# A two-block transformer kernel: the end and the start of the experts' weight stream reordered, and its last slabs cut into several transfers

## The reference

```python
def _moe(h, router_w, router_b, w_gate, b_gate, w_up, b_up, w_down, b_down):
    logits = (h @ router_w + router_b)                 # 256 x 32 experts
    top_logit, top_e = lax.top_k(logits, TOP_K)        # 4 experts for a token
    top_w = jax.nn.softmax(top_logit, axis=-1)
    ...
    def expert_block(args):
        xe, e = args
        gate = jnp.minimum(xe @ w_gate[e] + b_gate[e], 7.0)
        up = jnp.clip(xe @ w_up[e] + b_up[e], -7.0, 7.0)
        act = (up + 1) * (gate * jax.nn.sigmoid(1.702 * gate))
        return act @ w_down[e] + b_down[e]
    ...
    y = yb[dest] * sorted_w[:, None]
    return jax.ops.segment_sum(y, sorted_tok, num_segments=t)
```

## Time and profile before

| what | value |
|---|---|
| median of 3 runs | 1879.58 us (1879.22 to 1886.42) |
| the profiled execution, first to last instruction | 1879.4 us |
| TensorE busy | 1788.0 us, 95% |
| VectorE busy | 669.4 us, 36% |
| ScalarE busy | 575.4 us, 31% |
| transfers | 563.18 MB, 300 GB/s over the span |
| chain that ended last | PE 76%, DMA 18%, DVE 3%, ACT 2% |

### The profile page before, as it was taken

One profiled execution on the slowest core, in us unless ns is written; L12 is line 12 of the kernel. 1 busy time (PEld: TensorE's weight loads), 2 busy tenths in 40 slices (PEclk: granted clock), 3 DMA queues, 4 the chain that ended last, 5 costly groups with the idle time before them and its releaser, 6 DMA issues.

```text
span 1879.4 us, 24354 instructions
## 1 busy us (share of the span) xinstructions
PE 1788.0 (95%) x10246; PEld 1086.8 (58%) x10246; DVE 669.4 (36%) x1211; ACT 575.4 (31%) x1042; POOL 20.1 (1%) x59
## 2 busy tenths in 40 slices
PE   5999999999999999999999999989999999989999
PEld 4987787333333333333323233268799997779998
DVE  2654664111111111111111111154655455655454
ACT  4445573101101100110101011045554445555443
POOL 0010010000000000000000000000000000000000
PEclk9999999999999999999999999999999999999999
DMA  8664547999999999999999999974455464325450
GB/s 308 242 218 174 192 180 319 407 427 426 427 428 427 427 428 426 426 427 428 428 427 427 427 426 428 427 284 157 135 173 186 159 220 143 128 90 189 170 202 23
DMA packets 122048, 563.18 MB, mean 300 GB/s; under 512 B 7216, under 2 KB 53424, under 8 KB 97360
## 3 DMA queue, kind: packets, MB, share of 16 engines
q1 hardware_dynamic: 121104, 558.70, 74.4%
q10 hardware_dynamic: 832, 2.89, 0.4%
HBM read 560.52 MB, written 1.05 MB: 299 GB/s over the span
## 4 chain that ended last, share of the span: by engine, by line
PE 76%; DMA 18%; DVE 3%; ACT 2%; issue 1%; SPq 0%; ACTq 0%; DVEq 0%
PE ps L1093 15%; PE ps L660 12%; PE ps L661 12%; PE ps L662 12%; PE ps L1116 10%; DMA arena<-in_w_up 9%; DMA ring<-in_w_up 7%; PE ps L1051 2%; PE ps L1031 2%; DMA ring<-in_w_ada 1%; PE ps L672 1%; PE ps L979 1%; DMA ring<-in_w_in 1%; PE ps L765 1%; PE ps L1012 1%
## 5 line engine op out<-in xcount | busy, mean ns | idle before, releaser
L660 PE MATMUL ps<-part,part 128*128 128x256 f32 (+2 forms) x1592 | 512.0, 322 | 7.9 <-DVE part L1998 5.0
L661 PE MATMUL ps<-part,part 128*128 128x256 f32 (+2 forms) x1592 | 502.0, 315 | 0.0
L662 PE MATMUL ps<-part,part 128*128 128x256 f32 (+2 forms) x1592 | 501.7, 315 | 0.0
L1998 DVE TENSOR_TENSOR part<-ring,part 128x1024 fp32r<-128x1024 f32 (+2 forms) x299 | 313.2, 1089 | 122.4 <-ACT part L1455 121.8
L660 PEld LDWEIGHTS ps<-part,part 128*128 128x128 f32 (+1 forms) x1592 | 304.3, 191 | 42.0 <-issue 13.6
L662 PEld LDWEIGHTS ps<-part,part 128*128 128x128 f32 (+1 forms) x1592 | 304.0, 191 | 19.3
L661 PEld LDWEIGHTS ps<-part,part 128*128 128x128 f32 (+1 forms) x1592 | 304.4, 191 | 17.1
L1455 ACT ACTIVATE part<-ring 128x1024 fp32r<-128x1024 f32 (+2 forms) x299 | 271.9, 948 | 34.6 <-PE ps L662 18.9
L1093 PE MATMUL ps<-ring,arena 128*64 128x512 f32 x1216 | 269.9, 595 | 10.9 <-DMA ring<-in_w_up 9.4
L1995 DVE TENSOR_SCALAR arena<-ps 128x512 f32<-128x512 f32 x64 | 44.2, 691 | 428.1 <-PE ps L1093 428.1
L1093 PEld LDWEIGHTS ps<-ring,arena 128*64 128x64 f32 x1216 | 84.2, 137 | 193.7 <-issue 169.1
(11 more groups left out here) (254 smaller groups left out, 1218.0 us busy)
## 6 DMA issues: line engine op xcount, KB each, us to landing
ring<-in_w_down SPq DMA_DIRECT2D x39, 2048.0 KB, 35.6
ring<-in_w_up SPq DMA_DIRECT2D x38, 2048.0 KB, 36.0
ring<-in_w_gate SPq DMA_DIRECT2D x38, 2048.0 KB, 35.0
arena<-in_w_up SPq DMA_DIRECT2D x26, 2048.0 KB, 36.9
ring<-in_ffn_w_in SPq DMA_DIRECT2D x44, 1024.0 KB, 7.8
arena<-in_w_down SPq DMA_DIRECT2D x18, 2048.0 KB, 37.0
spare<-in_w_gate SPq DMA_DIRECT2D x13, 2048.0 KB, 35.4
arena<-in_w_gate SPq DMA_DIRECT2D x13, 2048.0 KB, 34.7
```

Of the source, the lines that this page charges most:

```text
L660: e.matmul(out, x[0], y[0], start=first, stop=False, skip_group_check=True)
L661: e.matmul(out, x[0], y[1], start=False, stop=False, skip_group_check=True)
L662: return e.matmul(out, x[1], y[0], start=False, stop=last, skip_group_check=True)
L1998: return e.tensor_tensor(out, x, y, op)
```

## The change

- **First slab.** 0.g0 raises `s_used` four times, once for each of its four rows of weights (k = 0 to 3), and the load that takes its slot, 1.d0, is four transfers of one row each (128 partitions of 4 KB, 512 KB), each waiting for its row.
- **Order.** Expert 31's g0, u0, g4, u4 are loaded before expert 30's d0 and d4, and PE runs them in that order: for expert 30, `turn_act` is followed by `turn_gathered(31)` and all of `gate_up(31)`, then by d0 and d4. DVE evicts expert 30's down result after expert 31's activation. Expert 31's gate and up slabs count on a signal of their own.
- **Last slabs.** 31.g4, 31.u4 and 31.d0 are each loaded as five transfers: one of 96 partitions and four of 8 partitions. 31.d4 is four transfers of one row each, with a signal for each, and PE waits for each row by itself.
- **`begin_sum`** moves from expert 0 to expert 27, behind `put_back(26)`; the first `put_back` starts the sums in its place.

```diff
@@ plan_rows
             src = w[128 * k0:128 * k0 + 512, :].rearrange("(p k) n -> p k n", k=4)
-            plan(key, 4, D, lambda ap: [(ap, src)], slot)
+            n = 1 if user[slot] == first_used or key == last_used else 4
+            if key in (("moe_g", NE - 1, 4), ("moe_u", NE - 1, 4), ("moe_d", NE - 1, 0)):
+                cuts = (0, 96, 104, 112, 120, 128)
+                plan(key, 4, D, lambda ap: [(ap[x:y], src[x:y]) for x, y in zip(cuts, cuts[1:])], slot)
+                return
+            plan(key, 4, D, lambda ap: [(ap[:, k:k + n, :], src[:, k:k + n, :]) for k in range(0, 4, n)], slot)
@@ order of the loads
         for ex in range(NE):
+            if ex < NE - 1:
+                plan_gate_up(ex)
+            if ex == NE - 2:
+                plan_gate_up(NE - 1)
             for k0 in (0, 4):
                 plan_rows(("moe_d", ex, k0), A["w_down"][0][ex], k0, next(order))
@@ sync_program
-                for to, src in pairs:
-                    e.dma_start(to, src).then_inc(s_slot[slot].sem, 16)
+                for n, (to, src) in enumerate(pairs):
+                    if before == first_used:
+                        e.wait_ge(*s_used.of("gate", 0, n))
+                    e.dma_start(to, src).then_inc(s_last_row[n].sem if key == last_used else s_slot[slot].sem, 16)
@@ tensor_program
+                    if ex < NE - 1:
+                        gate_up(ex)
                     if ex:
                         put_back(ex - 1)
                     else:
-                        begin_sum()
+                        e.wait_ge(*s_pickTe.of())
+                    if ex == 27:
+                        begin_sum(False)
                     if ex + 1 < NE:
                         gather(ex + 1)
                     turn_act(ex)
+                    if ex == NE - 2:
+                        turn_gathered(NE - 1)
+                        gate_up(NE - 1)
                     for k0 in (0, 4):
                         w = ("moe_d", ex, k0)
-                        if k0 and ex + 1 < NE:
+                        if k0 and ex + 1 < NE - 1:
                             turn_gathered(ex + 1)
                         e.wait_ge(*s_ate.of(ex, k0 // 4))
-                        e.wait_ge(*loaded(w))
+                        if w != last_used:
+                            e.wait_ge(*loaded(w))
                         for k in range(4):
+                            if w == last_used:
+                                e.wait_ge(s_last_row[k].sem, 16)
@@ vector_program
+                    if ex == NE - 1:
+                        e.wait_ge(*s_put.of(ex - 2))
+                        e.wait_ge(*s_used.of("down", ex - 1, 4))
+                        evict_down(ex - 1)
```

More of the change, by code:

```diff
@@ L223, in plan @@
             pairs = pairs_of(ap)
-            in_slot[slot] += 16 * len(pairs)
+            if key != last_used:
+                in_slot[slot] += 16 * len(pairs)
             loads.append((key, pairs, slot, user[slot]))
@@ L258, in build, with used, using @@
         s_slot = [signal(f"slot{i}_loaded", 16) for i in range(NSLOT + 4)]
-        s_used = signal("weights_used")
+        s_last_row = [signal(f"last_row{k}_loaded", 16) for k in range(4)]
+        s_used, s_used_end = signal("weights_used"), signal("last_gate_up_used")
+        def used(kind, ex, k0):
+            return (s_used_end if ex == NE - 1 and kind != "down" else s_used).of(kind, ex, k0)
+        def using(kind, ex, k0):
+            return (s_used_end if ex == NE - 1 and kind != "down" else s_used).up(kind, ex, k0)
         def W(key):
@@ L426, in build, with plan_gate_up @@
         user[7], user[8], user[9] = ("tiles", 7), ("tiles", 8), ("tiles", 9)
-        for ex in range(NE):
+        def plan_gate_up(ex):
             for k0 in (0, 4):
@@ L431, in build @@
                     plan_rows(("moe_u", ex, k0), A["w_up"][0][ex], k0, next(order))
+        for ex in range(NE):
+            if ex < NE - 1:
+                plan_gate_up(ex)
+            if ex == NE - 2:
+                plan_gate_up(NE - 1)
             for k0 in (0, 4):
@@ L621, in rel @@
                 return [s_wlo.of("a", max(t for t, x in enumerate(a_pieces) if x[0] == key))]
-            if kind in ("moe_g", "moe_u"):
-                return [s_used.of("gate" if kind == "moe_g" else "up", key[1], key[2])]
-            if kind == "moe_d":
-                return [s_used.of("down", key[1], key[2])]
+            if key == first_used:
+                return []
+            if kind in ("moe_g", "moe_u", "moe_d"):
+                return [used({"g": "gate", "u": "up", "d": "down"}[kind[-1]], key[1], key[2])]
             return [s_wlo.of(last_of[key])]
@@ L991, in turn_weights, with begin_sum @@
                 i.then_inc(*s_pickT.up())
-            def begin_sum():
+            def begin_sum(first):
                 e.wait_ge(*s_pickTe.of())
@@ L998, in begin_sum @@
                     for h in range(2):
-                        e.matmul(b.Y[q][h], b.wT[:, 128 * q:128 * q + 128], bdn[:, 512 * h:512 * h + 512], start=True, stop=False,
+                        e.matmul(b.Y[q][h], b.wT[:, 128 * q:128 * q + 128], bdn[:, 512 * h:512 * h + 512], start=first, stop=False,
                                      skip_group_check=True)
@@ L1082, in tensor_program, with project @@
                     xg, aT = b.xg, b.aT
[L1083 to L1089 removed]
+                    def project(n, r, k0):
+                        w, bank = ("moe_" + "gu"[r], n, k0), (6 if n % 2 == 0 else 4) + r
                         e.wait_ge(*loaded(w))
@@ L1092, in project, with gate_up @@
                             for h in range(2):
-                                i = e.matmul(PS[p + r][CAP * h:CAP * h + CAP, :], xg[:, k0 + k, :],
+                                i = e.matmul(PS[bank][CAP * h:CAP * h + CAP, :], xg[:, k0 + k, :],
                                              W(w)[:, k, 512 * h:512 * h + 512], start=False,
                                              stop=k0 == 4 and k == 3, skip_group_check=True)
-                        i.then_inc(*s_used.up(("gate", "up")[r], ex, k0))
-                    for k0 in (0, 4):
-                        for r in range(2):
-                            project(r, k0)
+                            if w == first_used:
+                                i.then_inc(*s_used.up("gate", 0, k))
+                        if w != first_used:
+                            i.then_inc(*using(("gate", "up")[r], n, k0))
+                    def gate_up(n):
+                        e.wait_ge(*s_xge.of(n))
+                        if n:
+                            e.wait_ge(*s_pwe.of(n))
+                            biases(n)
+                        for k0 in (0, 4):
+                            for r in range(2):
+                                project(n, r, k0)
+                    if ex < NE - 1:
+                        gate_up(ex)
                     if ex:
@@ L1124, in tensor_program @@
                 turn_weights()
-                begin_sum()
+                begin_sum(True)
                 for h in range(2):
@@ L2390, in vector_program @@
                         w = ("moe_d", ex, k0)
-                        e.wait_ge(*loaded(w))
+                        if w != last_used:
+                            e.wait_ge(*loaded(w))
+                        else:
+                            for k in range(4):
+                                e.wait_ge(s_last_row[k].sem, 16)
                         tt(W(w), W(w), b.gm.unsqueeze(1).to_broadcast([128, 4, D]), ALU.mult).then_inc(*s_dclip.up("down", ex, k0))
```

31 lines of the change are left out of this document (14 added, 17 removed).

## The result

The changed kernel takes **1916.2 us** (1911.76 to 1919.72, 4 runs) for 1881.0 of the kernel before in the same comparison (1879.22 to 1886.42): ratio **1.0173**, interval 1.0151 to 1.0194. It is 1.7% slower. Forecast were 1875.3, with 1879.7 as the upper end.

What follows compares the result with a forecast made beforehand. Slab transfers were taken to set the time from mid-stream to its end. 4.3 us from the stream plus 0.7 from the order minus 0.7 lost behind gave 1879.6 - 4.3 = 1875.3 us, range 1871.0 to 1879.7.

Steps and rivals of the forecast that it cites:

- The cuts of 96 and 8: Last slabs 31.g4, 31.u4, 31.d0: small pieces shift packets between engines, landings up to 3.7 us sooner or later; PE gains nothing.
- The small pieces cost, slower: Rival, last stretch: twelve small transfers each hold the queue 2.8 us, 31.d0 lands 33.6 later; 1907 us, chance 0.05.
- What would show it: List of signs in the trace; a rate well under 427 GB/s from 1190 to 1225 would mean pieces that cost.
- begin_sum: Moved from expert 0 to 27: later slots come free 3.3 us sooner at the front; cost 0 at expert 27.
- the stream's 4.3: Experts' weight stream: with both early gaps in the landings closed, it is 4.3 us sooner; bounds 2.8 to 5.6.
- First slab by rows: Start of the stream: 1.d0 issued row by row, 2.75 us sooner; landings of 1.d4, 2.g0, 2.u0 move by 1.4 us.
- The last slabs' order: End of the MoE: PE's idle time falls from 2.86 to 2.2 us, gain 0.7; the end then bound by PE.

Runs made afterwards that it cites:

- first ladder: Changed kernel with whole last slabs and one up slab cut at each of eight experts, a different shape each; one execution took 1963.6 us.
- experiment 10: Three kernels; the one for `begin_sum` is the kernel before with only that sum moved from expert 0 to expert 27: 1878.4 us, ratio 0.9987.
- experiment 1: Changed kernel with 31.g4, 31.u4 and 31.d0 loaded whole again, all else of the change kept: 1881.52 us, ratio 0.9996.
- experiment 7: Changed kernel with whole last slabs and six up slabs cut: every fourth, eighth, sixteenth partition, a middle piece, 112 + 16, halves; 1961.74 us.
- experiment 8: Changed kernel with whole last slabs and up slab 0 of six experts each cut into two halves of 64 partitions: 1936.45 us.
- the ladders: Two runs of the changed kernel with whole last slabs and single up slabs cut in eight, then six, shapes: 1963.6 and 1961.74 us.

## Why the prediction was wrong

- **"The cuts of 96 and 8"** is the step that failed. It counted packets, two more or two less for an engine and slab, and put 0 us into the forecast. It took for granted that a packet takes the same 0.61 us in whatever pieces the slab is cut. In the trace the engines stayed busy and moved half, at 1.27 us a packet. Measured: 34.7 us (1916.2 - 1881.5, from two comparisons whose kernels before are 1.8 apart), the whole loss.
- **The rival "The small pieces cost, slower"** had the side and, by chance, the size (1907, 32 us), from a wrong mechanism: a fixed time for each piece. Halves without a small piece cost 25.9 us, sixteen small pieces in the first ladder no more than two large ones. It got 0.05, because landings 4.9 us apart "for whole transfers" were held against it. That row says nothing of transfers that aren't whole, and there was none in the trace: a missing row was read as a price of 0. The bound from above had to come from this rival, and the range should have reached to it.
- **What would show it** named the sign rightly: "a rate well under 427 from 1190 to 1225".
- ***begin_sum*** moved the later issues nearly as foretold (2.g4 is issued 21.4 us behind g0, foretold 21.1, before 24.4), and at expert 27 cost nothing visible. What came of it at the end of the MoE is less than the stream's 4.3: 2.5 us in its own kernel (experiment 10).
- ***First slab by rows***: foretold 1.4 us, measured 0 to 0.1. In experiment 1 the four rows are issued from 324.15 to 326.72, 4.2 to 7.8 us ahead of their landings, and the last is in at 326.72 + 7.8 = 334.5, where the whole slab landed at 334.6. 1.d4 then lands 9.4 us after its issue at 330.15, at 339.6 for 339.5. The forecast had it land after 7.7. Without these 1.4 the forecast's front is 4.3 - 1.4 = 2.9 us; from g0 to the landing of 30.u4 the stream gained 2.8 (see the result).
- ***The last slabs' order***: foretold 0.7, measured 0.2 with the rows of 31.d4. PE's wait for ACT came as foretold (0.96 for 0.95). But the end isn't "bound by PE then": in experiment 1 PE still waits 1.24 us for 30.d4, as it did for 31.u4 before. The forecast's sum had no landing in it there (30.d4 was to be in at 1220.4 "at the worst", for a PE that would come later). The wait moved to another slab.
- **The whole without the cuts** gains 912.4 - 910.0 = 2.4 us in experiment 1's profile, for 4.3 in the forecast; its median is 1.2 under its comparison's, which can't be told from 0.

What stays open: whether the packets slow at the writing side, as the ports have it, or at the reading side (experiment 7), and why a cut into halves costs more than its own slab at half rate (4.9 us; measured 6.6 to 18.9). Transfers beside it that are whole slow down too (31.u0 and 30.d4 in the result), and the price rises from cut to cut (experiment 8). Engines that stand at different places of the queue, so that each slows another's whole transfer, would do both; that 31.u0 is late, though it stands ahead of every cut slab, fits it. The records don't name a packet's engine or partition, so this is argued, not shown.

## What to carry to other kernels

If a transfer into SBUF (the core's memory of 128 partitions) has to be cut, cut it along its free axis, within the partitions, or take every second or fourth partition; a cut into runs of partitions cost 7 to 19 us a slab of 2 MB here, in a queue that was the bound. When a rate halves while the engines' share stays at 1, the packets have become slower: look at what they hold, and not for gaps or fixed costs. And where a shape of transfer has no row in the trace, its price is unknown and not 0: the range has to reach to the worst rival, however small its chance.

## What the runs showed of the hardware

- A transfer of every fourth partition costs nothing extra, every eighth 6.5 us a slab of 2 MB, every sixteenth 17.0, at an engine share of 1.0 in each.
- Pieces of one row (128 partitions x 4 KB) are free in the middle of the stream (425 GB/s), and gain nothing at its dry start.
- The price of a cut depends on the cuts before it: 6.6 to 11.0 us over six alike, and 11.9 and 18.9 in the ladders.
- Whole slabs beside cut ones are late too: 31.u0, ahead of the first cut slab, landed 9.4 us behind 31.g0, and 30.d4 10.7 us behind 30.d0, instead of 4.9.
- After waits of 6 to 7 us of PE for slabs its granted clock was 0.66 in the stretch, between 1.2 and 2.4 GHz; a slab's 16 matmuls then took 5.4 to 6.4 us for 3.65.
